# A two-layer fp32 backbone: the second layer's first MLP product made of seven block products

## The chip, the core and the metric

The kernel runs on one core of a Trainium2 chip. The metric is the device time of one execution in microseconds (us): the median of three runs of the kernel before is 2430.54 us (2429.8 to 2430.73). A matrix product runs on TensorE (PE in the rows; PEld is its weight load), elementwise work on VectorE (DVE), ScalarE (ACT) and GpSimd (POOL); SyncE (SP) issues most transfers.

## The reference

Two layers work on 1024 latent tokens of width 1024, with 256 context tokens beside them in the first. Each layer has a token mixer (Fourier mixing in layer 0, windowed attention in layer 1) and then a squared-ReLU MLP. Only layer 1's MLP is computed in a new way; it has no context tokens.

```python
def _sq_relu_mlp(h, w1, w2):
    return jnp.square(jax.nn.relu(h @ w1)) @ w2     # w1: 1024 x 4096, w2: 4096 x 1024
...
h_lat = h_lat + g2 * _sq_relu_mlp(_modulate(_rms_norm(h_lat, norm2_g[i]), sh2, sc2), mlp_w1[i], mlp_w2[i])
```

Everything is fp32. Each operand of a product is split into a rounded high part and the rest (`h` and `l` in the names), and a product is three matmuls: high by high, high by low, low by high (`mm3`, L51 to L53). ScalarE makes the high part with a copy; VectorE or GpSimd makes the low part with a subtraction (`lo_part`, L58).

## The kernel before

`layer_tail` runs for both layers: it projects the mixer's output (`project`, weights `l_ph`, `l_pl`), adds it to the residual `ht`, normalises into `nh` and `nl`, and runs the MLP. The tokens stand in two blocks of 512 (b = 0, 1), in layer 0 also a block of 256 context tokens. The 4096 hidden columns are taken in 16 pairs of 128-column chunks. For one pair:

- hidden: four units, each one chunk of w1 by one token block, 8 steps over the width of three matmuls with 512 columns: 24 matmuls a unit, 96 a pair. A unit's result stands in a PSUM bank `l_z_ps`. ScalarE takes the positive part into `l_slot` (`relu`, L953), VectorE multiplies it by the bank's positive part (`square`, L1254).
- outputs: the second product is already a seven-product (Strassen-Winograd) scheme. The 2 x 2 blocks are w2's two row chunks and its two halves of columns against the hidden blocks B11, B12, B21, B22. VectorE makes the sums of w2 (`summed`, L1291) and the differences T1 to T4 of the hidden blocks (`diff`, L1268), ScalarE and VectorE split them (`high` L964, `low` L58 into `l_al`). A product is 4 groups of three matmuls (L1589 to L1591), 84 matmuls a pair; group m writes the PSUM bank `l_yy_ps`m.
- read-out: the running sum in `l_yy_ps` is read after each product. Banks 0 to 2 are read by VectorE (`acc`, L1275), bank 3 by ScalarE (`side_read`, L971) and then added by GpSimd (`add`, L862). The next product's group m waits until bank m has been read (`freed`).

So there is one product of time between a group and its successor on the same bank. Each engine runs its own list in the order in which it is written (the bodies below `@block.vector` and so on), and waits on semaphores. In layer 1 the order of the products is M5, M3, M1, M6, M7, M4, M2, with M5 before the last hidden unit, B21.

In layer 0 GpSimd's list for a pair is `outputs(p, more)`: add M5, the low part of S2, add M3, the low part of w1's chunk 0 (`low1`), the low part of S3, add M2, add M1, the low parts of A22 and A21, `low1` of chunk 1, then the adds of M6, M7 and M4. The context product (`l_yc_ps`) in four groups waits for weight low parts; its third group, ahead of M4, needs those of A22 and A21. SyncE's list is `pair(r, ...)`: w1 chunks of the next pair, the six ada transfers of this pair (`load_a`, each released by a step of VectorE), w2 of the next pair, two ada transfers of the next.

## Time and profile before

| | |
|---|---|
| median of the runs | 2430.54 us |
| span of the profiled execution, first to last instruction | 2428.1 us |
| around the span, median less span | 2.4 us |
| PE / DVE / ACT / POOL busy | 94% / 72% / 45% / 42% |
| stage of layer 0's MLP | about 321 to 1165 us, 16 pairs |
| stage of layer 1's MLP | about 1750 to 2426 us, 16 pairs |

The page shows each engine's busy share over 40 slices and TensorE's granted clock in tenths. It is read from the top: who is full, where, and at which clock; then the timeline of single engines within one pair of each layer, which repeats.

### The profile page before, as it was taken

The page shows a single profiled execution, that of the slowest core. Times are in us where ns is not written, and L with a number is a line of the kernel's source. Part 1 is how long each engine was busy: PE and PEld are TensorE (multiplying, and loading weights), DVE is VectorE, ACT ScalarE, POOL GpSimd, SP SyncE. Part 2 cuts the span into 40 slices and gives each one's busy share as a digit, 9 for nine tenths or more (in the row PEclk, how much of TensorE's full clock was granted, in tenths as well). Part 3 has the DMA queues.
Part 4 walks back from the last instruction along what each step waited for, and adds up shares of the span by engine and source line. Part 5 has one row for each costly group of instructions (what it writes and reads, how often), then busy time and mean ns, then how long its engine had stood idle before and what let it go on. Part 6 is the DMA issues. An engine that isn't in the chain of part 4 may idle for free. (4 is left out here: it accounts for less than half of the span.)

```text
span 2428.1 us, 36937 instructions
## 1 busy us (share of the span) xinstructions
PE 2281.3 (94%) x11598; PEld 1900.3 (78%) x11598; DVE 1736.5 (72%) x2835; ACT 1100.7 (45%) x1985; POOL 1022.5 (42%) x816
## 2 busy tenths in 40 slices
PE   5989979999999999999699799888999999999998
PEld 3768868888888888888687677766778888888887
DVE  5653787777777777777774688871688787878776
ACT  5553443333333333333443588882343444444443
POOL 0003623433333443333656476765435353545443
PEclk9999999999999999999799899999999999999999
DMA  7434112222222222222212211104111111121212
GB/s 272 176 130 174 66 35 70 86 87 72 84 78 69 70 82 98 69 80 88 105 53 109 81 36 34 35 22 191 44 35 53 51 46 57 37 67 35 69 35 96
DMA packets 79297, 192.75 MB, mean 79 GB/s; under 512 B 6896, under 2 KB 15472, under 8 KB 75888
## 3 DMA queue, kind: packets, MB, share of 16 engines
q1 hardware_dynamic: 76288, 184.92, 22.4%
q10 hardware_dynamic: 2928, 6.82, 0.8%
q8 instruction: 42, 0.69, 0.1%
q14 instruction: 39, 0.32, 0.0%
HBM read 174.94 MB, written 16.78 MB: 79 GB/s over the span
## 5 line engine op out<-in xcount | busy, mean ns | idle before, releaser
L862 POOL TENSOR_TENSOR ht<-ht,l_side 128x512 f32<-128x512 f32 x224 | 301.3, 1345 | 919.2 <-ACT l_side L971 910.8
L1275 DVE SCALAR_TENSOR_TENSOR ht<-l_yy_ps,mod,ht 128x512 f32<-128x512 f32 x672 | 466.1, 743 | 26.9 <-PE l_yy_ps L1591 26.0
L51 PE MATMUL l_z_ps<-nh,l_w1h 128*128 128x512 f32 (+1 forms) x1280 | 474.2, 370 | 11.7 <-DVE nl L1215 6.3
L52 PE MATMUL l_z_ps<-nl,l_w1h 128*128 128x512 f32 (+1 forms) x1280 | 473.2, 370 | 0.0
L53 PE MATMUL l_z_ps<-nh,l_w1l 128*128 128x512 f32 (+1 forms) x1280 | 472.6, 369 | 0.0
L1589 PE MATMUL l_yy_ps<-l_ah,l_w2h 128*128 128x512 f32 x896 | 355.6, 397 | 9.8 <-DVE ht L1275 6.9
L1590 PE MATMUL l_yy_ps<-l_al,l_w2h 128*128 128x512 f32 x896 | 351.0, 392 | 0.0
L1591 PE MATMUL l_yy_ps<-l_ah,l_w2l 128*128 128x512 f32 x896 | 350.5, 391 | 0.0
L971 ACT ACTIVATE l_side<-l_yy_ps,mod 128x512 f32<-128x512 f32 x224 | 154.1, 688 | 335.2 <-PE l_yy_ps L1591 335.2
L51 PEld LDWEIGHTS l_z_ps<-nh,l_w1h 128*128 128x128 f32 x1280 | 242.4, 189 | 54.5 <-issue 7.6
L53 PEld LDWEIGHTS l_z_ps<-nh,l_w1l 128*128 128x128 f32 x1280 | 242.5, 189 | 40.7
L52 PEld LDWEIGHTS l_z_ps<-nl,l_w1h 128*128 128x128 f32 x1280 | 242.5, 189 | 40.6 <-issue 0.5
L964 ACT ACTIVATE l_ah<-l_slot 128x512 fp32r<-128x512 f32 x224 | 141.6, 632 | 232.3 <-DVE l_slot L1254 93.4
L58 DVE TENSOR_TENSOR l_al<-l_slot,l_ah 128x512 fp32r<-128x512 f32 x224 | 185.8, 829 | 58.5 <-ACT l_ah L964 56.6
L1589 PEld LDWEIGHTS l_yy_ps<-l_ah,l_w2h 128*128 128x128 f32 x896 | 169.4, 189 | 50.3 <-DVE ht L1275 9.8
L1591 PEld LDWEIGHTS l_yy_ps<-l_ah,l_w2l 128*128 128x128 f32 x896 | 169.1, 189 | 36.4
L1590 PEld LDWEIGHTS l_yy_ps<-l_al,l_w2h 128*128 128x128 f32 x896 | 169.7, 189 | 31.8
L945 ACT ACTIVATE l_w2h<-l_w2f 128x512 fp32r<-128x512 f32 x240 | 141.7, 621 | 101.0 <-DVE l_w2f L1291 90.2
L2303 POOL TENSOR_TENSOR sc<-sc,den 128x640 f32<-128x640 f32 (+1 forms) x128 | 149.6, 1202 | 89.3 <-DVE den L2385 89.3
L58 POOL TENSOR_TENSOR l_w1l<-l_w1f,l_w1h 128x1024 fp32r<-128x1024 f32 x64 | 168.0, 2626 | 0.0
L58 POOL TENSOR_TENSOR l_w2l<-l_w2f,l_w2h 128x512 fp32r<-128x512 f32 x112 | 152.7, 1369 | 3.6 <-ACT l_w2h L945 3.5
L58 POOL TENSOR_TENSOR l_pl<-early,l_ph 128x1024 fp32r<-128x1024 f32 x20 | 49.4, 2473 | 247.9 <-ACT l_ph L1025 247.9
(250 smaller groups left out, 4515.5 us busy)
## 6 DMA issues: line engine op xcount, KB each, us to landing
l_aw<-ada SPq DMA_DIRECT2D x128, 256.0 KB, 2.9
l_w1f<-w SPq DMA_DIRECT2D x64, 512.0 KB, 3.5
l_w2f<-w SPq DMA_DIRECT2D x64, 512.0 KB, 4.9
maw<-ada SPq DMA_DIRECT2D x24, 1024.0 KB, 5.3
queries<-qhl SPq DMA_DIRECT2D x16, 512.0 KB, 2.8
stage<-queries SPq DMA_DIRECT2D x32, 256.0 KB, 2.7
early<-fnet_w SPq DMA_DIRECT2D x11, 512.0 KB, 4.5
early<-wo SPq DMA_DIRECT2D x11, 512.0 KB, 3.5
```

Of the source, the lines that this page charges most:

```text
L51: pe.matmul(out, lh, rh, start=first, stop=False)
L52: pe.matmul(out, lh, rl, start=False, stop=False)
L53: return pe.matmul(out, ll, rh, start=False, stop=last)
L58: return eng.tensor_tensor(lo, full, f32(hi), ALU.subtract)
L862: pool.tensor_tensor(h, h, side[(i - 1) % 2][:], ALU.add).then_inc(s_add, 1)
L945: act.activation(w2h[:, RING[name]], w2f[:, PLACE[name]], ACT.Copy).then_inc(s_w2h, 1)
L971: act.activation(side[(i - 1) % 2][:], y_ps[SIDE][:], ACT.Copy, scale=mod[:, layer, G2, m, 0:1]).then_inc(s_ya, 1)
L1275: dve.scalar_tensor_tensor(out=h, in0=y_ps[m][:], scalar=mod[:, layer, G2, c, 0:1], in1=h, op0=ALU.mult, op1=ALU.add).then_inc(s_acc, 1)
L1589: pe.matmul(y_ps[m][:], wh, a_h, start=first, stop=False, skip_group_check=not first)
L1590: pe.matmul(y_ps[m][:], wh, a_l, start=False, stop=False, skip_group_check=not first)
L1591: pe.matmul(y_ps[m][:], wl, a_h, start=False, stop=True, skip_group_check=not first).then_inc(s_y, 1)
L2303: pool.tensor_tensor(row, row, den[:, i, h:h + 1].to_broadcast(list(row.shape)), ALU.mult).then_inc(s_p, 1)
```

## The change

Layer 1's tail is a new function, `strassen_tail`. Its pairs 0 and 1 make the hidden blocks plainly, as before (`plain_block`). In pairs 2 to 15 the hidden product too is seven block products: the blocks are w1's two chunks by the two halves of the width, against the normalised tokens' halves of width and their two blocks. Each product is 4 steps of three matmuls, 12 matmuls, 84 a pair.

- The sums of layer 1's w1 and w2 are made during layer 0's MLP by transfers between DRAM tensors into the new tensor `sums`: in each of layer 0's 16 pairs SyncE issues four copies of 512 KB (`start_sums`), and GpSimd issues four transfers that add to their destination (`first_sums` twice, `more_sums` S2 and S4), with waits on the copies and on each other.
- The sums of the tokens are made once, in pair 1, on VectorE (16 instructions, `third_sum`, `first_sum`, `second_sum`, `fourth_sum`), and split (`high_t`, `low_t`: 16 on ScalarE, 12 on VectorE, 4 on GpSimd).
- The hidden products run in the order M1, M5, M6, M2, M7, M3, M4, accumulate in three banks, are copied by ScalarE in between (`copied`: 3 a pair) and summed by VectorE into PSUM (`zsum`: 3 a pair). The squared blocks and differences stand partly in PSUM, so that their low parts are read from there.
- The second product runs in the order M1, M6, M7, M4, M5, M3, M2, all of it after the hidden products. VectorE makes three of its seven low weight parts, GpSimd four; its sums are loaded, not made.

```diff
+            Z_ORDER = ["M1", "M5", "M6", "M2", "M7", "M3", "M4"]
+            Y_ORDER = ["M1", "M6", "M7", "M4", "M5", "M3", "M2"]
...
+                def first_sums(p):
...
+                    pool.wait_ge(s_sc, p * 64 + 64)
+                    pool.dma_start(sums[0, 0:2, to]..., w1[1, one, 1]..., accum_op=ALU.add, max_dma_last_dim=2048).then_inc(s_s1, 16)
+                    pool.dma_start(sums[1, 0:2, to]..., w2[1, chunks, :, 512:1024]..., accum_op=ALU.add, max_dma_last_dim=2048).then_inc(s_s1, 16)
...
+                def more_sums(p, name):
...
+                    if name == "S2":
+                        pool.wait_ge(s_s1, p * 32 + 32)
...
                     add(p, "M3")
+                    if C:
+                        first_sums(p)
                     if more and C:
                         low1(p + 1, 0)
                     low2(p, "S3")
                     for prod in ROWS[2:]:
                         add(p, prod)
+                        if C and prod in ("M2", "M7"):
+                            more_sums(p, "S2" if prod == "M2" else "S4")
...
+                if C:
+                    pool.wait_ge(s_s4, 16 * PAIRS)
...
+                def group(p, i, m):
...
+                    if m == SIDE:
+                        pe.wait_ge(s_ya, p * 7 + (PRE + i))
+                    else:
+                        pe.wait_ge(s_acc, p * 21 + (PRE + 3 * i + m - 2))
...
+                def last_sums(p, side_sums):
+                    diff(p, "T2")
+                    diff(p, "T3")
+                    low(p, "T2")
+                    low(p, "T3")
+                    acc(p, 0, 0)
+                    acc(p, 0, 1)
+                    if not (type(p) is int and p == 0):
+                        square(p, "B21")
+                    diff(p, "T4")
+                    low(p, "T1")
+                    acc(p, 0, 2)
+                    low(p, "T4")
+                    acc(p, 1, 0)
+                    low(p, "B22")
+                    acc(p, 1, 1)
+                    acc(p, 1, 2)
+                    acc(p, 2, 0)
+                    low(p, "B21")
...
+                def pair(p):
+                    for i in (0, 1, 2):
+                        low2(p, i)
+                    zsum(p, "B11")
+                    square(p, "B11")
+                    low(p, "B11")
+                    zsum(p, "B22")
+                    square(p, "B22")
+                    zsum(p, "B12")
+                    square(p, "B12")
+                    diff(p, "T1")
+                    last_sums(p, False)
```

## Rows read from the trace of the kernel before

**Rows 1.** The page: busy time by engine; granted clock in 40 slices.

```profile
PE 2281.3 (94%) x11598; PEld 1900.3 (78%) x11598; DVE 1736.5 (72%) x2835; ACT 1100.7 (45%) x1985; POOL 1022.5 (42%) x816
PEclk9999999999999999999799899999999999999999
```

**Rows 2.** Stretches: length, busy us of each engine (instructions), PEclk, DMA share, GB/s.

```profile
350.00:1090.00 740.00, 734.08 (x3887) 634.12 (x3888) 561.21 (x899) 268.71 (x446) 268.54 (x182) 1.00 0.24 78
1862.00:1903.00 41.00, 41.00 (x182) 33.77 (x181) 32.08 (x45) 17.04 (x28) 19.08 (x12) 1.00 0.15 51
```

**Rows 3.** Timeline, PE in layer 1: start us, duration us, instruction.

```profile
1863.34 0.39 PE L51 MATMUL l_z_ps<-nh,l_w1h 128*128 128x512 f32 x1
1864.02 0.39 PE L51 MATMUL l_z_ps<-nh,l_w1h 128*128 128x512 f32 x1
```

**Rows 4.** Timeline, DVE, a pair of layer 1: start, duration, idle before.

```profile
1859.37 0.74 DVE L1275 SCALAR_TENSOR_TENSOR ht<-l_yy_ps,mod,ht 128x512 f32<-128x512 f32 x1
...
1898.31 0.69 DVE L1254 SCALAR_TENSOR_TENSOR l_slot<-l_z_ps,l_slot 128x512 f32<-128x512 f32 x1 [1.60 <-ACT l_slot L953]
1899.04 0.69 DVE L1268 TENSOR_TENSOR l_slot<-l_slot 128x512 f32<-128x512 f32 x1
...
1900.31 0.74 DVE L1275 SCALAR_TENSOR_TENSOR ht<-l_yy_ps,mod,ht 128x512 f32<-128x512 f32 x1
1900.97 0.68 DVE L1268 TENSOR_TENSOR l_slot<-l_slot 128x512 f32<-128x512 f32 x1
1901.57 0.68 DVE L58 TENSOR_TENSOR l_al<-l_slot,l_ah 128x512 fp32r<-128x512 f32 x1
...
1903.50 1.40 DVE L58 TENSOR_TENSOR l_al<-l_slot,l_ah 128x512 fp32r<-128x512 f32 x1
1907.08 2.06 DVE L1275 SCALAR_TENSOR_TENSOR ht<-l_yy_ps,mod,ht 128x512 f32<-128x512 f32 x3
```

**Rows 5.** Timeline, ACT, the same pair: positive part, high part, side read.

```profile
1905.84 0.60 ACT L953 ACTIVATE l_slot<-l_z_ps 128x512 f32<-128x512 f32 x1 [2.42 <-PE l_z_ps L53]
1907.20 0.63 ACT L964 ACTIVATE l_ah<-l_slot 128x512 fp32r<-128x512 f32 x1 [0.76 <-PE l_yy_ps L1591]
```

**Rows 6.** Timeline, POOL in layer 1: an add and a low part.

```profile
1903.06 1.29 POOL L862 TENSOR_TENSOR ht<-ht,l_side 128x512 f32<-128x512 f32 x1 [17.19 <-ACT l_side L971]
1904.31 1.73 POOL L58 TENSOR_TENSOR l_w2l<-l_w2f,l_w2h 128x512 fp32r<-128x512 f32 x1
```

**Rows 7.** Timeline, PE at layer 1's first pair; a stretch behind its wait.

```profile
1777.15 0.47 PE L1589 MATMUL l_yy_ps<-l_ah,l_w2h 128*128 128x512 f32 x1 [2.94 <-DVE l_al L58]
1778.60:1781.70 3.10, 2.73 (x7) 1.61 (x5) 3.00 (x6) 2.24 (x4) 0.00 (x0) 0.51 0.00 0
```

**Rows 8.** Timeline, POOL in a pair of layer 0, and the next pair's first.

```profile
841.65 1.30 POOL L862 TENSOR_TENSOR ht<-ht,l_side 128x512 f32<-128x512 f32 x1 [31.88 <-ACT l_side L971]
...
845.40 2.90 POOL L58 TENSOR_TENSOR l_w1l<-l_w1f,l_w1h 128x1024 fp32r<-128x1024 f32 x1
849.49 2.76 POOL L862 TENSOR_TENSOR ht<-ht,l_side 128x512 f32<-128x512 f32 x2
852.20 2.56 POOL L58 TENSOR_TENSOR l_w2l<-l_w2f,l_w2h 128x512 fp32r<-128x512 f32 x2
895.00 1.30 POOL L862 TENSOR_TENSOR ht<-ht,l_side 128x512 f32<-128x512 f32 x1 [31.88 <-ACT l_side L971]
```

**Rows 9.** Timeline, PE in that pair: the third context group starts.

```profile
856.61 0.28 PE L51 MATMUL l_yc_ps<-l_ach,l_w2h 128*128 128x256 f32 x1
```

**Rows 10.** Transfers: an issue on SP; sizes and us to landing; a wait.

```profile
857.64 0.33 SPq L767 DMA_DIRECT2D l_w1f<-w  x1
l_w2f<-w SPq DMA_DIRECT2D x64, 512.0 KB, 4.9
881.95 0.75 DVE L1242 SCALAR_TENSOR_TENSOR l_side<-l_aw,l_sseq,l_side 128x512 f32<-128x512 f32 x1 [0.87 <-DMA l_aw<-ada]
```

More of the change, by code:

```diff
@@ L58, in lo_part, with hybrid_kernel @@
     return eng.tensor_tensor(lo, full, f32(hi), ALU.subtract)
-def hybrid_kernel(nc, x, ctxt, vecs, ada0, ada1, w1, w2, fnet_w, wqkv, wo, qkg, sink, dft, rope, masks, eye, out, park, qd):
+def hybrid_kernel(nc, x, ctxt, vecs, ada0, ada1, w1, w2, fnet_w, wqkv, wo, qkg, sink, dft, rope, masks, eye, out, park, qd, sums):
     ctx = ExitStack()
@@ L70, in sem @@
             return s
+        s_sums = [ctx.enter_context(nc.semaphore(n)) for n in ("sums13", "sums2", "sums4")]
         def recycle_semaphores():
@@ L561, in layer_tail @@
 def layer_tail(nc, sem, sb, banks, layer, wp, early, s_pw, w1, w2, mod, meanw, eps, ident, nh, nl, ht,
-               x=None, ctxt=None, g1b=None, ada1=None, vec=None, svec=None, ones=None, kv=None, sqs=None, park=None, out=None):
+               x=None, ctxt=None, g1b=None, ada1=None, vec=None, svec=None, ones=None, kv=None, sqs=None, sums=None, s_sums=None, park=None, out=None):
     PAIRS = DFF // (2 * P)
@@ L2561 @@
     qd = nc.dram_tensor("queries", (QB, HEADS // 4, P, 4 * 2 * HD), F32, kind="Internal").ap()
-    hybrid_kernel(nc, *args, out, park, qd)
+    sums = nc.dram_tensor("sums", (2, 4, 1 + DFF // (2 * P), P, 512), F32, kind="Internal").ap()
+    hybrid_kernel(nc, *args, out, park, qd, sums)
     r = run_bass_kernel_spmd(nc, [arrays], core_ids=[0])
```

903 lines of the change are left out of this document (901 added, 2 removed).

## The prediction

> **What bounds the kernel now.** I read the page's busy shares first: TensorE is busy for 94% of the span and its clock is near full nearly everywhere [rows 1]. Then the stretches: in both MLP stages TensorE has no idle time to speak of (734 of 740 us in layer 0, 41.0 of 41.0 in layer 1) at a granted clock of 1.00, its higher level, 2.4 GHz [rows 2]. So in both stages every microsecond that TensorE loses is a microsecond of the kernel, and every matmul less is a gain only as long as nobody else makes TensorE wait. In layer 1 three matmuls start within 0.68 us, 0.2267 each [rows 3], and a pair repeats after 1900.31 - 1859.37 = 40.94 us [rows 4]: 180 x 0.2267 = 40.81 and 0.13 of rest. VectorE is next, busy 32.1 of 41 [rows 2]. A page of shares hides the order within a pair, so I then followed each engine's timeline through a pair, since the change rearranges just that.
>
> **What the change removes.** In pairs 2 to 15 the hidden product has 84 matmuls for 96: 12 x 0.2267 = 2.72 us a pair, 14 pairs, 38.1 us. That is the whole gain, and a pair would take 168 x 0.2267 = 38.08 us.
>
> **What it does to VectorE in layer 1.** VectorE had 44 instructions a pair (21 read-outs, 7 low parts of operands, 4 squares, 4 differences, 4 weight sums, 4 weight low parts) and has 42 (three `zsum`, three weight low parts, the rest as before). Independent ones start 0.60 us apart (1900.97, 1901.57), a read-out takes 2.06/3, or 0.66 from the next, and one that needs its forerunner starts 0.73 behind it (1898.31, 1899.04) [rows 4]. 42 of them are some 27 us, so as a sum VectorE fits into 38 us. But their places have changed. Before, M5 ran between two hidden units, and the differences had that time. Now all hidden products come first, and M1, M6, M7, M4 follow without a gap, each group waiting for the read-out of the same bank one product (2.72 us) earlier.
>
> I work it through from the start of a pair's M1 (0). Product k of the hidden seven ends at 2.72k + 0.17 (a matmul ends 0.39 behind its start [rows 3]), and the next engine starts 0.03 later. The sixth, M3, ends at 16.49. Then VectorE `zsum` B12 16.52 to 17.21; ScalarE's positive part, 0.60 [rows 5], to 17.84; square to 18.56; T1 18.60; T2 19.32; T3 19.92; the high part of T2 on ScalarE, 0.63 [rows 5], to 20.67; low T2 20.70, low T3 21.30 to 21.98, first read-out 21.90 to 22.64. TensorE has finished M1's groups at 21.76 and can't start M6's first before 22.67: 0.9 lost. The second read-out ends at 23.30, in time. The third stands behind square B21 (23.2), T4 (23.9, behind it by dependence) and low T1 (24.5), and runs 25.15 to 25.89. M6's third group needed it at 24.03: 1.9 lost. Then low T4, read-out M6/0 to 27.15, low B22, read-out M6/1 to 28.41, where M7's second group needed it at 27.96: 0.5 lost. From M7's third group on the read-outs keep up (0.66 each against 0.68 a group). M4 starts at 30.48 where 27.20 was due, and the pair ends at 41.36. So the stall is 3.28 us and eats the 2.72: 41.36 - 40.94 = +0.42 a pair.
>
> VectorE's instructions that read and write PSUM both don't occur before; the nearest rows are those that read one operand from PSUM, 0.69 [rows 4]. I take these; 0.60 for each of the 13 in the chain (7.8 us and 1.2 for ScalarE's two) or 0.75 would make the pair 40.8 or 42. Where both its operands stand in SBUF, VectorE can be held by GpSimd: low parts take 1.40 for 0.69 now and then [rows 4], and GpSimd's 1.73 for 1.3 [rows 6]. Low T1 (24.5) falls on GpSimd's low part of M4's weights (about 23.5 to 24.8): +0.3, taken at half, +0.13. Layer 1's loop: 14 x 0.55 = +7.7 us (bounds -2 to +15).
>
> The Trainium skill (SBUF — State Buffer, Who interferes with whom) says that a VectorE instruction with two SBUF inputs contends with a GpSimd instruction that reads SBUF and one with at most one does not. The trace agrees, since read-outs from PSUM stay at 0.74 beside GpSimd. It speaks for blocks in PSUM, and leaves the order as it is.
>
> ScalarE (35 instructions, about 0.6 each, 22 us) and GpSimd (18, about 1.3, 24 us) fit into 41, their results each come over 1 us before they are needed, and w1's and w2's 14 transfers of 256 KB a pair are issued 3 us or more ahead of use: nothing.
>
> **Layer 1's first two pairs.** Pair 0 has lost 2.94 and two short waits, and then ran at 0.51 of the clock, the lower level, for 3.1 us [rows 7]. In the new order M1 can start at 1774.1, but the stall of the loop follows (4.6 us until M4): it ends near 1797.7, 1.6 earlier than now. In pair 1 VectorE has 16 token sums and 12 low parts more, 28 x 0.65 = 18 us. The sums fill its list to about 19 us, so that T2 and T3 come late: the first read-out ends at 28.3 where TensorE is ready at 24.5, the pattern above adds 2.4, and the low parts of T1 and T3 behind the read-outs of M4 and M5 add 0.6 and 1.7. +8.5 us (bounds +3 to +14, the latter if the clock falls once more). Layer 1 together: 7.7 - 1.6 + 8.5 = +14.6.
>
> **Layer 0.** GpSimd's list gets four transfers. None is issued by GpSimd in the trace, so their cost on it has bounds: 0.33 us, an issue on SyncE [rows 10], and 2.9, its longest instruction here [rows 8]. I take 1.3, an ordinary instruction of its own [rows 6]. From 841.65 GpSimd has no idle time until it has made A22 and A21 at 854.76; the third context group starts at 856.61 [rows 8, 9]. Slack 1.85 us. Three issues stand ahead (two behind M3's add, one behind M2's): 3.9 - 1.85 = 2.05 us a pair. TensorE is the bound, so it counts, in pairs 1 to 14 (pair 0 has idle time on GpSimd, pair 15 no `low1`): 29 us. In front of the third issue GpSimd waits for the first two to land. The second is issued until 848.1; GpSimd gets there at 848.1 + 5.4 = 853.5, so 5.4 us are covered; a plain load of this size lands in 4.9 [rows 10]. An addition moves three times for two, so it may take up to 9.8, and the wait 0 to 4.4; I take 0. Behind the wait stand the adds, which free the side buffers two products later, and A22 and A21. SyncE's four copies cost it 1.6 us and put 2 MB ahead of the next w1 chunk, which has 20 us; they would hit the ada transfers, for which VectorE waits 0.87 already [rows 10], only if they lasted over 14 us. At the end GpSimd waits for the last S4: +3 us. Layer 0 together +32 (bounds +3 to +130).
>
> The Trainium skill (DMA: Bandwidth & Descriptors, Specifications) puts the first byte of a transfer issued by GpSimd at about 1 us; by that estimate three issues less the slack are 1.15 a pair, 16 us for the 29. No row of this trace shows it.
>
> **Sum.** The profiled execution's span is 2428.1, and 2.4 us lie around it, against the median of 2430.5. 2428.1 + 14.6 + 32 + 2.4 = 2477 us.
>
> **Rivals.**
> Forecast: VectorE's list takes back the seven products' gain, and GpSimd's issues cost layer 0 29 us. 2477, chance 0.33.
> Cheap issues: an issue takes under 0.6 us on GpSimd and lies in the slack. For it: SyncE's 0.33. Against: GpSimd does nothing else in under 1.2. 2430.5 + 14.6 + 3 = 2448, chance 0.21.
> Late landings: the additions land in about 8.4 us, 3 us of wait for each of 14 pairs on top, 42 us. For it: each reads two sources and writes DRAM, beside w1's and w2's loads. 2519, chance 0.18. The clock belongs here too: stalls of 3 us have cost it before [rows 7], mine are at most 1.9 each.
> Faster: TensorE stays full in layer 1's loop. Its place is M6's third group, and it decides where the third read-out ends, 23.9 and not 25.9. Then 14 x 2.72 = 38 is kept, pair 1 costs 4, layer 0 its 3: 2430.5 - 38 - 1.6 + 4 + 3 = 2398. For it: VectorE's total fits with 11 us to spare, layer 0 may be free. Against: 13 instructions in 7 us were never seen. Chance 0.22.
> The change does the seven products, but a cheaper stall (2.7 in place of 3.3, pair 1 at +3) and free issues just cancel: 2431, chance 0.06.
>
> **How the numbers follow.** Likeliest is 2477. The range goes from the faster rival's time to just over the late landings, 2396 to 2525; beyond it lie late landings with the full 9.8 us and a faster case without pair 1's loss. Faster by over 0.2% (4.9 us, about what a measurement can tell from no change) 0.22, within 0.06, slower 0.72. The likeliest side's own range is 2440 to 2525.
>
> **What would show it.** In the loop of layer 1: a period of 41.4 to 41.6 us (38.1 by the faster rival), waits of TensorE at the second product's second, third and fourth group sets for VectorE's `ht` of about 0.9, 1.9 and 0.5 us, and VectorE without idle time from `zsum` B12 to M4's read-outs. In layer 0: a period over the 53.35 of now [rows 8] by 2 us, and a wait of TensorE at the third context group for GpSimd's low parts. If layer 0's period stays 53.35 the issue price was wrong; if layer 1's falls under 40, the order of VectorE's chain was.

## The result and the profile after

The changed kernel takes 2566.3 us (median of four runs, 2564.0 to 2568.6), the kernel before 2430.2 (2429.5 to 2430.7): 1.0555 times as long, 95% interval 1.054 to 1.057. The direction was forecast, the size was not: 136 us slower, where 47 had been worked out and 2525 us was the end of the range.

The page of the kernel after, the rows that answer to [rows 1] (span; busy us of an engine, share, instructions; granted clock in 40 slices):

```profile
span 2567.1 us, 38476 instructions
PE 2319.5 (90%) x11430; PEld 1908.2 (74%) x11430; DVE 1731.1 (67%) x2827; ACT 1155.4 (45%) x2117; POOL 1155.5 (45%) x974
PEclk9999989999999999999889899999989999999999
```

TensorE has 168 matmuls fewer in the list, is busy for longer all the same (2319.5 us for 2281.3) and has 101 us more of idle time. A busy time that rises with fewer instructions means a slower clock. So two things are to be found, waits and half clock, and the first question is in which stage.

The last projection matmul (tile l_ph) starts at 1743.4 in the trace of before and at 1829.5 in that of after: 86.1 us are lost before layer 1's MLP begins, and the remaining 139.0 - 86.1 = 52.9 in it. The stretches, as in [rows 2] (length, busy us and instructions of PE, PEld, DVE, ACT, POOL, then clock, DMA share, GB/s). First layer 0's MLP and one of its pairs, then a pair of layer 1:

```profile
350.00:1230.00 880.00, 830.02 (x4216) 707.90 (x4215) 614.80 (x979) 290.84 (x483) 345.59 (x255) 0.96 0.53 141
828.80:887.08 58.28, 55.47 (x285) 47.25 (x284) 40.70 (x66) 19.31 (x33) 22.98 (x17) 0.97 0.55 144
2074.80:2118.60 43.80, 40.46 (x170) 32.43 (x169) 29.70 (x42) 20.28 (x35) 23.43 (x18) 0.96 0.27 84
```

A pair of layer 0 takes 58.28 us where 53.35 stood [rows 8], and it was forecast at 55.4. A pair of layer 1 takes 43.8 where 40.94 stood [rows 4], and 41.5 was forecast. In both the clock is no longer 1.00. The pair shown is one of the shorter: layer 0's fourteen loop pairs take 58.0 to 60.1 us, 58.60 in the mean, and make 73 of the 86 us. Layer 1's (42.9 to 44.0, mean 43.80) make 40 of the 53.

**A pair of layer 0, GpSimd** (start us, duration, instruction, idle time before it and what ended it), to be laid beside [rows 8]:

```profile
832.55 1.03 POOL L909 DMA_DIRECT2D sums<-w  x1
833.29 1.46 POOL L910 DMA_DIRECT2D sums<-w  x1
834.00 3.19 POOL L58 TENSOR_TENSOR l_w1l<-l_w1f,l_w1h 128x1024 fp32r<-128x1024 f32 x1
836.37 2.06 POOL L58 TENSOR_TENSOR l_w2l<-l_w2f,l_w2h 128x512 fp32r<-128x512 f32 x1
837.62 2.06 POOL L881 TENSOR_TENSOR ht<-ht,l_side 128x512 f32<-128x512 f32 x1
841.88 1.15 POOL L922 DMA_DIRECT2D sums<-sums  x1 [2.20 <-DMA sums<-w]
842.64 1.70 POOL L881 TENSOR_TENSOR ht<-ht,l_side 128x512 f32<-128x512 f32 x1
843.88 2.90 POOL L58 TENSOR_TENSOR l_w2l<-l_w2f,l_w2h 128x512 fp32r<-128x512 f32 x2
```

An issue holds GpSimd for about 0.74 us (832.55, 833.29, 834.00), not the 1.3 of the sum. But the third stands behind 2.20 us of waiting for the first two to land (1.9 to 3.1 in the fourteen pairs), and only behind it come the low parts of A22 and A21. The transfers in this stage (count, size of each, median us to landing):

```profile
sums<-w POOLq DMA_DIRECT2D x30, 512.0 KB, 7.3
sums<-sums POOLq DMA_DIRECT2D x30, 512.0 KB, 6.0
l_w2f<-w SPq DMA_DIRECT2D x30, 512.0 KB, 4.2
```

An addition lands in 7.3 us, a load of the same size in 4.2. TensorE's timeline in the same pair, at its two waits:

```profile
844.08 0.50 PE L1635 MATMUL l_yy_ps<-l_ah,l_w2h 128*128 128x512 f32 x1 [0.84 <-ACT l_side L1017]
847.03 0.36 PE L51 MATMUL l_yc_ps<-l_ach,l_w2h 128*128 128x256 f32 x1 [1.97 <-POOL l_w2l L58]
```

The second is the wait for GpSimd's low parts, for which the landing wait stands in front. The first has another cause, which ScalarE's and SyncE's rows show. TensorE waits for a side read-out, and ScalarE, which reads it, has first waited 2.75 us for the load of w1's second chunk:

```profile
842.40 1.06 ACT L984 ACTIVATE l_w1h<-l_w1f 128x1024 fp32r<-128x1024 f32 x1 [2.75 <-DMA l_w1f<-w]
843.36 0.67 ACT L1017 ACTIVATE l_side<-l_yy_ps,mod 128x512 f32<-128x512 f32 x1
837.35 0.33 SPq L771 DMA_DIRECT2D l_w1f<-w  x1
l_w1f<-w SPq DMA_DIRECT2D x1, 512.0 KB, 5.0
```

The same load in the pair of before that starts at 841.65, where ScalarE doesn't wait for it (its copy starts at 852.40):

```profile
848.46 0.33 SPq L767 DMA_DIRECT2D l_w1f<-w  x1
l_w1f<-w SPq DMA_DIRECT2D x1, 512.0 KB, 3.4
```

Both chunks use one buffer, so this load is issued when GpSimd has made chunk 0's low part (`load1` waits for it). That low part stands behind the first two issues: the load goes out 8.55 us behind the pair's first GpSimd instruction, where it was 6.81. And it lands in 5.0 us, not 3.4, beside the additions. Together it comes 3.3 us later. ScalarE had 0.5 us to spare for it; TensorE, further down, about 2.3, since 1.0 of the 3.3 reaches it.

The stretch behind the second wait (columns as above):

```profile
849.00:851.50 2.50, 2.50 (x7) 1.92 (x7) 1.63 (x3) 0.00 (x0) 2.36 (x3) 0.50 1.04 371
```

The gap between starts is 1.00 us over the usual 0.23 at the first wait and 2.14 at the second. From 848.2 on three narrower matmuls (256 columns) start 0.17 to 0.22 apart, not 0.12, six of 512 columns 0.43 apart and a seventh 0.37, not 0.23: 1.6 us more, since the granted clock is 0.50, the lower level of 1.2 GHz. With two starts that are 0.1 late behind a wait this is 4.9, the whole 4.93 of the pair.

**A pair of layer 1, VectorE** from the `zsum` of B12 on. Its pair's first matmul started at 2070.66:

```profile
2087.48 0.70 DVE L2452 TENSOR_TENSOR l_z_ps<-l_z_ps,l_slot 128x512 f32<-128x512 f32 x1
2088.84 0.69 DVE L2459 SCALAR_TENSOR_TENSOR l_slot<-l_z_ps,l_slot 128x512 f32<-128x512 f32 x1 [0.66 <-ACT l_slot L2177]
2089.57 0.69 DVE L2469 TENSOR_TENSOR l_slot<-l_z_ps,l_slot 128x512 f32<-128x512 f32 x1
2090.29 0.69 DVE L2473 SCALAR_TENSOR_TENSOR l_slot<-l_slot,l_z_ps 128x512 f32<-128x512 f32 x1
2090.90 0.69 DVE L2476 TENSOR_TENSOR l_z_ps<-l_z_ps,l_slot 128x512 f32<-128x512 f32 x1
2091.68 0.69 DVE L58 TENSOR_TENSOR l_al<-l_slot,l_ah 128x512 fp32r<-128x512 f32 x1
2092.29 0.68 DVE L58 TENSOR_TENSOR l_al<-l_z_ps,l_ah 128x512 fp32r<-128x512 f32 x1
2092.89 1.40 DVE L2491 SCALAR_TENSOR_TENSOR ht<-l_yy_ps,mod,ht 128x512 f32<-128x512 f32 x2
2094.20 0.69 DVE L2462 SCALAR_TENSOR_TENSOR l_z_ps<-l_z_ps,l_slot 128x512 f32<-128x512 f32 x1
2095.00 0.69 DVE L2480 SCALAR_TENSOR_TENSOR l_z_ps<-l_slot,l_z_ps 128x512 f32<-128x512 f32 x1
2095.61 1.50 DVE L58 TENSOR_TENSOR l_al<-l_slot,l_ah 128x512 fp32r<-128x512 f32 x1
2097.03 0.74 DVE L2491 SCALAR_TENSOR_TENSOR ht<-l_yy_ps,mod,ht 128x512 f32<-128x512 f32 x1
```

(The square of B22 stands at 2086.65, just ahead of it.) And TensorE, which waits for the read-outs in the first and the last `ht` row above:

```profile
2093.85 0.49 PE L2662 MATMUL l_yy_ps<-l_ah,l_w2h 128*128 128x512 f32 x1 [1.01 <-DVE ht L2491]
2097.82 0.79 PE L2662 MATMUL l_yy_ps<-l_ah,l_w2h 128*128 128x512 f32 x1 [2.33 <-DVE ht L2491]
```

The stretch behind the second:

```profile
2097.90:2100.90 3.00, 3.00 (x7) 2.40 (x8) 3.00 (x5) 0.11 (x1) 0.33 (x1) 0.50 0.47 175
```

Again by gaps between starts: 1.18 and 0.10 at the first wait, 2.48 at the second, and 0.36, five times 0.20 and 0.17 while the clock is 0.50, 1.5 us. Together 5.3, and 38.5 for the rest, the 168 matmuls' own 38.1 among them, make the period of 43.8. All pairs of the loop have these two waits, but two of thirteen have no half clock behind them:

```profile
2027.77:2070.66 42.89, 39.42 (x170) 31.20 (x168) 29.57 (x43) 20.27 (x35) 23.43 (x18) 1.00 0.28 86
```

So the half clock costs such a pair 1.1 us net (44.0 for 42.9): at full clock a third, shorter wait shows, which the half clock covers.

### The profile page after: what moved, and what is told of

It is laid out like the page before. It is cut to its first block and busy times, and to the rows that moved or that the text cites. A ratio compares the mean times of both kernels' runs of the same rounds, so it can differ in the third digit from the quotient of the medians.

```text
span 2567.1 us, 38476 instructions
## 1 busy us (share of the span) xinstructions
PE 2319.5 (90%) x11430; PEld 1908.2 (74%) x11430; DVE 1731.1 (67%) x2827; ACT 1155.4 (45%) x2117; POOL 1155.5 (45%) x974
## 5 line engine op out<-in xcount | busy, mean ns | idle before, releaser
L51 PE MATMUL l_z_ps<-nh,l_w1h 128*128 128x512 f32 (+1 forms) x816 | 292.9, 359 | 6.6 <-POOL l_w1l L58 3.4
L53 PE MATMUL l_z_ps<-nh,l_w1l 128*128 128x512 f32 (+1 forms) x816 | 291.8, 358 | 0.0
L52 PE MATMUL l_z_ps<-nl,l_w1h 128*128 128x512 f32 (+1 forms) x800 | 285.8, 357 | 0.0
L1321 DVE SCALAR_TENSOR_TENSOR ht<-l_yy_ps,mod,ht 128x512 f32<-128x512 f32 x336 | 235.9, 745 | 20.6 <-PE l_yy_ps L1637 19.2
L58 POOL TENSOR_TENSOR l_w1l<-early,l_w1h 128x512 fp32r<-128x512 f32 x104 | 135.6, 1311 | 179.7 <-ACT l_w1h L2149 179.7
L1635 PE MATMUL l_yy_ps<-l_ah,l_w2h 128*128 128x512 f32 x448 | 187.0, 417 | 22.3 <-ACT l_side L1017 14.6
L51 PEld LDWEIGHTS l_z_ps<-nh,l_w1h 128*128 128x128 f32 x816 | 154.8, 190 | 30.4 <-issue 4.0
L1017 ACT ACTIVATE l_side<-l_yy_ps,mod 128x512 f32<-128x512 f32 x112 | 76.6, 684 | 214.8 <-PE l_yy_ps L1637 214.8
L53 PEld LDWEIGHTS l_z_ps<-nh,l_w1l 128*128 128x128 f32 x816 | 154.9, 190 | 22.4
L52 PEld LDWEIGHTS l_z_ps<-nl,l_w1h 128*128 128x128 f32 x800 | 152.0, 190 | 22.0 <-issue 0.5
L2662 PEld LDWEIGHTS l_yy_ps<-l_ah,l_w2h 128*128 128x128 f32 x448 | 90.1, 201 | 97.1 <-DVE ht L2491 58.4
L2491 DVE SCALAR_TENSOR_TENSOR ht<-l_yy_ps,mod,ht 128x512 f32<-128x512 f32 x192 | 136.3, 745 | 24.2 <-PE l_yy_ps L2664 24.2
```

Source lines behind the costliest of these rows:

```text
L51: pe.matmul(out, lh, rh, start=first, stop=False)
L52: pe.matmul(out, lh, rl, start=False, stop=False)
L53: return pe.matmul(out, ll, rh, start=False, stop=last)
L58: return eng.tensor_tensor(lo, full, f32(hi), ALU.subtract)
L1321: dve.scalar_tensor_tensor(out=h, in0=y_ps[m][:], scalar=mod[:, layer, G2, c, 0:1], in1=h, op0=ALU.mult, op1=ALU.add).then_inc(s_acc, 1)
L1635: pe.matmul(y_ps[m][:], wh, a_h, start=first, stop=False, skip_group_check=not first)
```

## The experiments

After the traces I had this theory (P in the first four expectations): each stage loses by itself, layer 0 by where the additions stand in GpSimd's list, layer 1 by where the read-outs stand in VectorE's; the traffic of the sums as such costs little. The rivals: one stage disturbs the other, or the traffic and the issues cost whatever their place.

**sums_alone.** The additions as in the kernel after, layer 1's MLP as before (the sums are made and not used).

```diff
-        strassen_tail(..., w1, w2, sums, ...)
+        layer_tail(nc, sem, sb, banks, 1, wo, early, s_pw, w1, w2, ...)
```

> The kernel before with layer 0's sum transfers added, layer 1's MLP as before (the sums are not read). Theory P (what the trace of the changed kernel shows: in each middle pair of layer 0 TensorE waits behind GpSimd, which itself waits 2.2 us for the first additions to land; the pair goes from 53.35 to 58.28 us; the two stages are independent): 15 x 4.93 plus the end of the layer, 86 us up to the last projection of layer 1, so 2430 + 86 = 2516 us, and layer 1's MLP as long as before. Rival I (the stages act on each other, for example through the clock or through what the transfers leave behind): under 2495 or over 2535 us.

Measured 2514.6 us, 1.034 of before (1.031 to 1.037): layer 0 costs 82 us by itself (before took 2432.6 beside it). The last projection matmul starts at 1831.2, as in the kernel after (1829.5).

**layer1_alone.** No copies and no additions; layer 1 with its seven products, which loads a plain block of the same size for each sum (so the weight sums are left out).

```diff
-                        start_sums(r)
...
-                        first_sums(p)
...
-                            more_sums(p, "S2" if prod == "M2" else "S4")
```

> The changed kernel without any sum transfers; layer 1 loads plain blocks of w1 and w2 of the same size in place of the sums, so what it computes in layer 1 leaves the sums of weights out. Theory P: layer 0 as before (53.35 a pair), layer 1's MLP as long as in the changed kernel, period 43.8, total 2430 + 51 = 2481 us. Rival I: layer 1's period falls clearly under 43 us, since the stall came from loads of the sums.

Measured 2482.6, 1.021 (1.018 to 1.024), and the last projection matmul starts at 1742.5, as before (1743.4). Layer 1 costs 50 us by itself, and 82 + 50 = 132 of the 136 for both. So the two parts are separate and can be explained one by one.

**first_only.** The first additions stay, S2 and S4 are left out.

```diff
-                        if C and prod in ("M2", "M7"):
-                            more_sums(p, "S2" if prod == "M2" else "S4")
```

> As sums_alone, but the two second-stage transfers (S2, S4) are left out: GpSimd issues only the two additions of the first stage and waits for nothing inside the pair. Theory P (it is the wait for the landing and the third issue that use up the slack of 1.85 us; an issue holds GpSimd 0.74 us): 2 x 0.74 = 1.5 us fits into the slack, layer 0's pair stays at 53.4, total 2430 to 2436 us. The prediction's price of 1.3 us an issue: 2.6 - 1.85 = 0.75 a pair, 2440 to 2446 us. Rival D (the DRAM traffic itself slows layer 0): the pair stays near 57 to 58 us, over 2490 us.

(The sums S2 and S4 are not made.) Measured 2464.9, 1.013 (1.011 to 1.016). Layer 1 is as before here too, so layer 0's cost falls from 82 to 32 us. That is none of the numbers expected. The trace shows two things. In an ordinary pair (period 54.5) TensorE waits 0.9 us for a side read-out (ScalarE l_side, 11.7 us in 13 waits), and ScalarE again waits for w1's second chunk first, which lands in 5.0 us (50.3 us of such waits in 14 pairs). And in 3 of the 16 pairs, the 4th, 8th and 11th, GpSimd's second issue is held:

```profile
920.56 1.02 POOL L909 DMA_DIRECT2D sums<-w  x1
926.69 1.15 POOL L910 DMA_DIRECT2D sums<-w  x1 [5.12 <-issue]
```

From one issue to the next it is 6.13 us where 0.73 is usual; such a pair takes 58.5 to 58.9 us for 54.5. Fourteen pairs at 1.1 and three holds at 4.2 are 29 of the 32 us. In the kernel after no pair has a hold: its second issue starts 0.73 to 0.87 behind the first in all 16. So the holds belong to this variant and are no part of the 136 us.

**first_small.** first_only with half the memory for GpSimd's descriptors.

```diff
-    nc = bacc.Bacc("TRN2", ..., dynamic_dma_scratch_size=4096)
+    nc = bacc.Bacc("TRN2", ..., dynamic_dma_scratch_size=2048)
```

> The kernel with the first additions alone (S2 and S4 left out, so these two sums are not made: part of the computation is missing), with the memory for GpSimd's transfer descriptors halved, 2048 bytes for 4096. In three of its sixteen pairs (the 4th, 8th and 11th) GpSimd's second issue was held for 5.1 to 5.5 us and the pair took 58.5 to 58.9 us for 54.5. Theory V (a new transfer has to wait for room among the descriptors of the one in flight): with half the room at least six pairs are held, 2465 rises by 4.3 for each, to 2478 or more, up to 2520 when every pair is. Rival (the hold has nothing to do with that memory): three holds again, 2461 to 2469.

Measured 2484.7, 1.021 (1.020 to 1.023): 20 us more, and six pairs held for three, by 5.2 to 5.7 us each (427.83, 541.19, 600.88, 769.84, 938.61, 1108.29). So the hold depends on that memory. More than 4096 bytes was not tried. Why the hold falls on the 8th, 16th and 22nd transfer, and why the kernel after has none, is open.

**second_later.** All transfers, but S2's issue behind the low parts of A22 and A21, and S4's behind the pair's last addition.

```diff
                         add(p, prod)
-                        if C and prod in ("M2", "M7"):
-                            more_sums(p, "S2" if prod == "M2" else "S4")
...
                         if prod == "M1":
                             for name in W_LATE[2:]:
                                 low2(p, name)
                             if more:
                                 low1(p + 1, 1 if C else 0)
+                            if C:
+                                more_sums(p, "S2")
+                    if C:
+                        more_sums(p, "S4")
```

> The kernel after, with GpSimd's issue of the second addition (S2) put behind the low parts of A22 and A21, and of the third (S4) behind the last addition of the pair; the same transfers in all. In the kernel after GpSimd waits 2.20 us there for the first additions to land and spends about 0.75 on the issue, all ahead of the low parts that TensorE waits 2.0 for. Theory L (what failed in the sum for layer 0 is the wait for landing, priced at nothing): the waits of TensorE for l_w2l vanish, the period of a pair of layer 0 falls from 58.28 to 54.4 to 55.6, where the kernel with the first additions alone stands (54.47), time 2566 less 38 to 54: 2512 to 2528. Rival I (the issues and the traffic themselves hold the pair, wherever they stand): period 57 or more, time over 2548.

Measured 2511.6, 1.033 (1.031 to 1.034): 54.8 us of the kernel after's 136 come back by moving two issues. In the trace the first additions have landed when GpSimd gets to S2 (873.63 in the pair below, without a wait), all waits of TensorE for l_w2l in the loop are gone, and the half clock with them in thirteen of fourteen pairs. TensorE's wait that is left:

```profile
871.84 0.50 PE L1637 MATMUL l_yy_ps<-l_ah,l_w2h 128*128 128x512 f32 x1 [0.89 <-ACT l_side L1019]
```

And the pair as a stretch:

```profile
860.27:914.79 54.52, 53.63 (x286) 46.09 (x285) 40.43 (x66) 19.37 (x32) 23.19 (x19) 1.00 0.57 154
```

3.76 us of the pair's 4.93 are gone (by the means of fourteen pairs 58.60 has become 54.93). On TensorE that is the second wait with its late start, 2.2, and the half clock, 1.6. The remaining 1.17 is the wait of 0.89 for l_side and its surroundings, with ScalarE waiting for w1's second chunk as in the kernel after (43.3 us in 14 pairs). The adds that free the side buffers are not the cause: the last add ahead of that read-out ends at 868.85, and ScalarE reads at 871.11, right behind its copy of the late chunk. The odd pair is of use for the clock: its one wait of 1.97 for l_side (982.10) has the half clock behind it, and the pair takes 57.1 us.

**sums_in_idle.** All issues where GpSimd has nothing to do, behind the pair's last addition; the copies behind the ada transfers. The last pair stays as it was.

```diff
-                    if C:
+                    if C and not more:
                         first_sums(p)
...
-                        if C and prod in ("M2", "M7"):
+                        if C and not more and prod in ("M2", "M7"):
                             more_sums(p, "S2" if prod == "M2" else "S4")
...
                     if more and not C:
                         low1(p + 1, 1)
+                    if more and C:
+                        first_sums(p)
+                        more_sums(p, "S2")
+                        more_sums(p, "S4")
```

> The changed kernel with layer 0's additions of a pair moved behind GpSimd's last add of that pair, where it stands idle for 32 us (the last pair as it was), and SyncE's copies moved behind the six ada transfers. All sums are made. Theory P (a matter of place, not of traffic): layer 0's pair back to 53.4 us, total within 6 us of layer1_alone, about 2485 us. Rival D (traffic): layer 0's pair stays over 56 us, total over 2525 us.

Measured 2496.8, 1.027 (1.024 to 1.030): 70 of the kernel after's 136 us are back, and 14 over layer1_alone stay, 12 over the time expected. GpSimd's third and fourth issue in a pair (the first two start at 923.27 and 924.01):

```profile
932.45 1.14 POOL L922 DMA_DIRECT2D sums<-sums  x1 [6.96 <-DMA sums<-w]
940.84 1.14 POOL L922 DMA_DIRECT2D sums<-sums  x1 [7.25 <-DMA sums<-sums]
```

A pair as a stretch:

```profile
901.87:955.22 53.35, 53.35 (x285) 46.19 (x284) 40.19 (x66) 19.31 (x33) 23.55 (x17) 1.00 0.59 157
```

In this pair and eight more of the fourteen the period is before's 53.35 [rows 8], with twice the bytes moved (157 GB/s for 79). GpSimd now waits 7 us twice and it costs nothing, and ScalarE waits for w1 nowhere: its second chunk is issued as early as before and lands in 3.6 us. So it was the place of issues and traffic that cost nearly all of it. The traffic isn't quite free: an ada transfer lands in 4.8 us for 2.9, VectorE's waits for l_aw double from 19.3 to 41.7 us in all, and five pairs are 0.4 to 1.2 us longer because TensorE waits for VectorE's ada step, 3.4 us together. The 14 us that stay are before layer 1 (last projection matmul at 1757.5, 14.1 behind before's): 3.5 up to the loop, 3.4 in it, and 7 behind it, of which 4.5 are the last pair's wait for l_w2l.

**third_read_early.** From here on the kernels are about layer 1. The third read-out of the first product right behind the second:

```diff
                     acc(p, 0, 1)
+                    acc(p, 0, 2)
                     if not (type(p) is int and p == 0):
                         square(p, "B21")
                     diff(p, "T4")
                     low(p, "T1")
-                    acc(p, 0, 2)
```

> The kernel after, with one operation of VectorE's order moved in layer 1's MLP: the third read-out of a pair's first product (l_yy_ps bank 2) is done right after the second, ahead of the last block's square, of T4 and of the low part of T1. In the kernel after the read-out starts 26.35 us behind the pair's first matmul and TensorE waits 2.33 for it; moved ahead of three operations of 0.60, 0.73 and 1.50 us it should start at about 23.5 and that wait be gone. Theory Q (VectorE's order sets the loop of layer 1, and the half clock follows the two waits): the period of the loop falls from 43.81 to between 40.3 and 42.0 (some of the three moved operations then make the third product late instead, 0.5 to 1.5 us), fourteen pairs and pair 1, so 2566 falls to 2515 to 2543. Rival R (the half clock at this place comes from something else than the second wait, the time of that wait only being given back later, at T4): the half clock stretch stays, the period is 42.5 or more, time over 2546. Rival N (the loop is set by GpSimd's low parts or loads): no change, 2560 to 2570.

Measured 2549.6, 1.048 (1.046 to 1.050): 17 us gained. That is outside what theory Q said, and both the time (over 2546) and the mean period (43.1, R said 42.5 or more) are R's. The trace explains it. The wait of 2.33 at M6's third group is gone, and one of 1.76 at M7's first group has come, for M6's first read-out, which still stands behind the square, T4 and the low parts of T1 and T4. And the clock does two different things in two successive pairs with the same waits (1.02 and 1.76 in one, 1.01 and 1.76 in the next):

```profile
2067.07:2110.90 43.83, 40.93 (x170) 32.45 (x169) 29.01 (x42) 20.16 (x35) 23.50 (x18) 0.96 0.28 84
2110.90:2153.39 42.49, 39.59 (x170) 31.34 (x169) 29.08 (x42) 20.16 (x35) 23.47 (x18) 1.00 0.28 86
```

43.83 against 42.49: the half clock costs 1.34 us by itself here. Over the loop, seven of thirteen pairs have it (43.6 to 44.0) and six don't (42.3 to 42.5).

**fill_waits.** The order of the kernel after, but TensorE multiplies low parts by low parts where it would wait.

```diff
                     pe.matmul(y_ps[m][:], wh, a_l, start=False, stop=False, ...)
+                    if not is_plain(p):
+                        for _ in range({(0, 3): 3, (1, 1): 9}.get((i, m), 0)):
+                            pe.matmul(y_ps[m][:], wl, a_l, start=False, stop=False, ...)
```

> The kernel after, with twelve more matmuls of 0.23 us (low parts times low parts, a term the kernel leaves out as too small to matter, repeated) in each pair of layer 1's loop: three at the end of the first product and nine in the second group of the second product, just where TensorE waits 1.01 and 2.33 us in the kernel after. They fill 0.68 of the first wait and 2.04 of the second, so nothing that TensorE waits for comes later. Theory Q (the half clock of 3 us follows from the waits): TensorE is busy in their place, the granted clock stays above 0.95 through the stretch, and the period falls from 43.81 by the 1.3 to 1.9 us that the half clock costs, to 41.9 to 42.5; fourteen pairs, 2566 falls to 2540 to 2548. Rival R (the half clock comes from elsewhere, for example from what all matmuls together draw): clock as before, period 43.8 or more, time 2564 to 2575; more matmuls would then even make it worse.

Measured 2552.5, 1.049 (1.047 to 1.051): 14 us faster with 168 matmuls more. A pair as a stretch:

```profile
2071.65:2114.55 42.90, 42.12 (x182) 33.44 (x181) 29.60 (x42) 20.39 (x35) 23.51 (x19) 1.00 0.28 85
```

Of its two waits on TensorE the first is 0.33 (2090.71) and the second:

```profile
2094.74 0.50 PE L2662 MATMUL l_yy_ps<-l_ah,l_w2h 128*128 128x512 f32 x1 [0.32 <-DVE ht L2491]
```

The clock stays at 1.00 in every pair of the loop, so the half clock does follow the waits. Both the time and the period are above what theory Q expected. The period is that of the kernel after's two pairs at full clock (42.9), so the gain is 1.1 us in each of the others and not 1.5, because at full clock TensorE reaches M7's groups earlier and meets another late read-out there (M7's second group, 0.53 behind its forerunner, 0.30 over the usual). In the kernel after, the half clock hides this third wait; the two pairs without it show it.

**reads_between.** VectorE's whole order dealt anew, T4's parts ahead of T1's, ScalarE's side read-out of M6 ahead of T4's high part; the same operations.

```diff
                     diff(p, "T2")
-                    diff(p, "T3")
-                    low(p, "T2")
-                    low(p, "T3")
                     acc(p, 0, 0)
+                    low(p, "T2")
                     acc(p, 0, 1)
+                    acc(p, 0, 2)
+                    diff(p, "T3")
+                    acc(p, 1, 0)
+                    low(p, "T3")
+                    acc(p, 1, 1)
+                    acc(p, 1, 2)
                     if not (type(p) is int and p == 0):
                         square(p, "B21")
                     diff(p, "T4")
...
```

> The kernel after, with VectorE's order in layer 1's MLP dealt anew: each read-out of the first three products stands ahead of the operation that the next product doesn't need yet (T2, read, low T2, read, read, T3, read, low T3, read, read, square, T4, read, low T4, read, read, low T1), T4's parts are made before T1's, and ScalarE reads the second product's side chunk before it makes the high part of T4. The same operations, all of them. Theory Q: with 0.60 to 0.70 us each, the first two products' groups find their banks read; the fourth product waits about 1.2 us for the low part of T4; period 39.5 to 40.8 in place of 43.81, 14 pairs, and 2 to 5 us in pairs 0 and 1: 2566 falls to 2503 to 2524. Rival W (the work of VectorE between the third block's square and the fourth product is too much in any order, and the waits only move): one wait of 2.5 us or more at the fourth product with half clock behind it, period 42 or more, time over 2540.

Measured 2525.5, 1.039 (1.038 to 1.041): 41 us gained, 1.5 short of what theory Q expected. M4's wait of 1.2 isn't there; another stands at M6's fourth group, for ScalarE. The period is 40.94 and the clock 1.00:

```profile
2063.52:2104.46 40.94, 39.32 (x170) 31.25 (x169) 29.24 (x42) 20.30 (x35) 23.36 (x18) 1.00 0.30 90
```

TensorE's largest wait in it:

```profile
2084.81 0.51 PE L2664 MATMUL l_yy_ps<-l_ah,l_w2h 128*128 128x512 f32 x1 [1.18 <-ACT l_side L2194]
```

**reads_between_idle** has both moves, this order and the additions in GpSimd's idle time.

> The last kernel (VectorE's order dealt anew in layer 1's MLP) with the additions of the sums put into GpSimd's idle time at the end of each pair of layer 0 and their copies behind the loads. If the two edits are in stages that don't touch each other, their gains add: 2497 (sums_in_idle) less what the new order alone gains against the kernel after (43 to 63 us expected): 2434 to 2454, no faster than the kernel before. If the order of layer 1 gains more than 66 us, the block products beat the kernel before (2430).

Measured 2457.3, 1.011 (1.009 to 1.013). From 2496.8 to 2457.3 are 39.5 us, from 2566.3 to 2525.5 are 40.8: the gains add, and before isn't reached.

**reads_between_idle2.** ScalarE's side read-out of the first product ahead of T3's high part.

```diff
                     high(p, "T2")
+                    side_read(p, 0)
                     high(p, "T3")
...
-                    side_read(p, 0)
```

> reads_between_idle with one more move: ScalarE reads the side chunk of a pair's first product (l_side) ahead of making T3's high part, which waits for VectorE. In reads_between TensorE waited 1.18 us in each pair of layer 1's loop for that read-out, the largest wait left there. If nothing else is late behind it: period 40.94 falls to 39.7 to 40.0, in 14 pairs 13 to 17 us, 2457 falls to 2440 to 2444, still slower than before. If the next wait (0.43 for VectorE's read-out) takes it over: 2448 or more.

Measured 2457.3, 1.011 (1.009 to 1.012): nothing. The period is 40.97, the wait of 1.18 for ScalarE is gone, and one of 1.03 for VectorE stands at M4's first group. The wait:

```profile
2015.90 0.50 PE L2668 MATMUL l_yy_ps<-l_ah,l_w2h 128*128 128x512 f32 x1 [1.03 <-DVE l_al L58]
```

The first and the last two of VectorE's instructions ahead of it, which have no idle time between them:

```profile
2005.68 0.69 DVE L2473 TENSOR_TENSOR l_slot<-l_z_ps,l_slot 128x512 f32<-128x512 f32 x1
...
2014.40 0.75 DVE L2495 SCALAR_TENSOR_TENSOR ht<-l_yy_ps,l_gneg,ht 128x512 f32<-128x512 f32 x1
2015.15 0.69 DVE L58 TENSOR_TENSOR l_al<-l_z_ps,l_ah 128x512 fp32r<-128x512 f32 x1
```

From T1 to T4's low part, which M4's first group needs, these are 15 instructions in 10.2 us (2005.68 to 2015.84), and TensorE is through with its own work 1.03 earlier. Each of the 15 is needed by M4's first group or by a group ahead of it, so an order within them can only move that wait. This is the second kernel in which it moved and the period stayed. Giving one of the 15 to another engine was not tried.

**last_pair_late.** The last pair's additions are moved to GpSimd's list in layer 1, behind pair 0.

```diff
-                    if C and not more:
-                        first_sums(p)
...
+                sp.wait_ge(s_sums[2], 16 * PAIRS)
                 with sp.Fori(PLAIN, PAIRS - 1) as p:
```

> reads_between_idle2 with the additions of the last pair (the one pair whose additions still stand among GpSimd's low parts in layer 0) done in layer 1 instead, in GpSimd's order behind pair 0; its sums are first loaded twelve pairs later. TensorE's wait of 4.5 us for l_w2l at the last pair of layer 0 should go, and some of the wait behind it: 4 to 8 us faster than reads_between_idle2, so 2433 to 2439, within 0.4% of before but not under it. If more than 8 us come back, it is level with the kernel before.

Measured 2449.3, 1.008 (1.006 to 1.009): 8 us faster than the last one, the upper end of the gain expected (the time expected was lower, as it built on the last one's). It is the best version with block products, 117 us faster than the kernel after, and the kernel before is still faster by 18.

## Why the prediction was wrong

By its own steps, the number forecast and the number found:

| step | forecast | found |
|---|---|---|
| issue on GpSimd | 1.3 each | 0.74 each (6.1 in three pairs of first_only, in none of the kernel after) |
| landing of the first additions | within 5.4 us, no wait | 7.3 median, a wait of 2.20 |
| w1's second chunk, ScalarE, side read-out | not in the sum | 3.3 us later, TensorE waits 0.84 |
| layer 0, a loop pair | +2.05 | +5.25 in the mean (+4.93 in the pair shown) |
| layer 0 in all | +32 (bounds +3 to +130) | +82 alone, +86 beside layer 1 |
| first read-out of M1's groups | 21.90 | 22.23 |
| third read-out | 25.15 | 26.37 |
| waits at M6's groups | 0.9 and 1.9 | 1.01 and 2.33 |
| clock behind them | full | 0.50 for 3 us, in 11 of 13 pairs |
| layer 1, a loop pair | +0.55 | +2.87 |
| layer 1 in all | +14.6 | +50 alone, +53 beside layer 0 |

**Mechanism and size.** The sign was right, and so was the mechanism in layer 1, the place of the read-outs. In layer 0 the engine was right, GpSimd's list, but not what in it costs: the sum had the three issues, and the trace has the wait between them, a second chain behind the first two, and the clock. The two terms came out 2.6 and 3.4 times as large. The steps that failed:

**The landing wait, taken as 0.** I had bounds of 0 to 4.4 and 5.4 us of cover. The additions of the pair above took until 841.9 with an issue at 833.3, 8.6 us. The cover was as forecast: GpSimd came to the wait 5.7 us behind the second issue's end. I took the end of the bounds that lies nearest to a plain load (4.9 us), though I had written down myself that an addition moves three times for two: 1.5 x 4.9 = 7.35 would have been the estimate, and 7.3 is what was measured. With it the wait is about 2 us (7.35 - 5.4), 27 us more for the sum: about 2504, an estimate by the prediction's own numbers and still 62 short. The rival of late landings (2519) named this mechanism; it had 0.18. second_later shows that it was the largest part of layer 0's loss: with the half clock behind it, 54.8 us came back.

**The issue price** was too high (1.3 for 0.74), an error the other way: three issues are 2.2 us, little more than the slack of 1.85. **The second chain** wasn't in the sum at all. I measured the slack of one consumer of GpSimd's list only, the low parts of A22 and A21 (1.85 us). Chunk 0's low part stands behind the first two issues as well, and on it hang the load of w1's second chunk, ScalarE's copy of it and the side read-out behind that copy. The load went out 1.7 us later and took 1.6 longer (5.0 for 3.4) beside the additions, and TensorE could bear about 2.3. By this estimate neither would have cost it anything alone, but no run parts the two. TensorE's 0.84 to 0.9 us stand in first_only and second_later too, and are gone in sums_in_idle, where neither stands ahead of the load.

The Trainium skill (DMA: Bandwidth & Descriptors, Specifications) gave about 1 us for a transfer's first byte by GpSimd. For what GpSimd itself is held the trace has 0.74; for the time until an addition of 512 KB has landed it has 6.0 to 7.3. The first number says nothing of either, and the estimate by it, 16 us for layer 0, was further off than the 29 from the rows.

**The clock** failed in both stages. I wrote that stalls of 3 us have cost it before and that mine are at most 1.9 each, and left it in a rival for layer 0 alone. In both stages the trace shows two waits within 4 us (0.84 and 1.97; 1.01 and 2.33) and then about 3 us at 0.50. In layer 0 all fourteen pairs have it (two of them for longer), and by the gaps between starts it costs about 1.7 us a pair, 24 us (an estimate from these gaps); second_later took the larger wait away, and the clock went back to 1.00 in all pairs but one. In layer 1 fill_waits kept VectorE's times, filled the waits, had 1.00 in every pair, and was 14 us faster. Together some 38 us that stood nowhere in the sum. It is no sharp rule of the waits' sizes: two pairs of layer 1 with the same waits kept the full clock, six of third_read_early with 1.0 and 1.8 too, while a single wait of 1.97 brought the half clock in a pair of second_later.

**VectorE's chain in layer 1** was followed rightly: seven operations after `zsum` B12, each came 0.3 us later than worked out, as `zsum` itself stood behind the square of B22 (2086.65, 2087.48), and operations that read and write PSUM take 0.69 to 0.70, the value taken. The term for the contention was too small. Low T1 fell on GpSimd's low part as forecast, and took 1.50 us in place of 0.69; I had taken half of 0.3. The Trainium skill (SBUF — State Buffer, Who interferes with whom) says that a VectorE instruction with two SBUF inputs contends with a GpSimd instruction that reads SBUF, and that one with at most one does not. The trace agrees: low T1, with slot and high part in SBUF, is the only one in the list above that is lengthened, and low T4 behind it, which reads PSUM, takes 0.68 (2097.69) although GpSimd's add runs beside it (2096.51, for 1.72). The rule names who is hit; it was for me to take the price from the row of before, 0.7 more [rows 4], in full.

The third wait, 0.5 in the sum, at M7, is there at 0.3, and most pairs of the kernel after don't show it: the half clock covers it. It appears as soon as the clock is full (fill_waits).

**The rivals.** Cheap issues (2448) had an issue under 0.6 us; 0.74 is nearer to it than to the sum's 1.3, but its result was wrong, since the wait for landing and the late load stand behind the issues. Faster (2398) hung on the third read-out's end; in third_read_early TensorE no longer waited for it, and the late group was another one. reads_between_idle2 shows why: the limit is the sum of VectorE's work in that stretch and not one read-out's place. So a kernel in which the seven products keep their 38 us didn't exist in any order of the same operations that I tried. The best loop of layer 1 has the period of before (40.94), with 12 matmuls less a pair, all of them turned into waits. That the two figures are the same is chance as far as the traces show: before, TensorE's matmuls filled the period; here they fill 39.3 us of it, and waits for VectorE and ScalarE the rest.

**What stays open.** Pairs 0 and 1 of layer 1, with the ends of the loop, have the remaining 53 - 40 = 13 us (waits of 6.24 and 3.91 for VectorE's read-outs in pair 1, half clock behind both); I had +6.9 for them and changed nothing there by itself. Of layer 0's 86 us 13 lie outside the loop's fourteen pairs, 4 up to it and 9 behind; last_pair_late gave back 8. How much of the late load is the issues' and how much the traffic's isn't parted. What makes the clock fall or stay in two like pairs isn't settled.

## What to carry to other kernels

Where a list of work goes on an engine behind a wait, price the wait and then every chain that hangs on the list behind it, not only the tightest one that comes to mind: here two low parts had 1.85 us of slack, and a third, which frees a load buffer that ScalarE's list waits for, had about 2.3, of which a slower transfer took 1.6. Some 18 us later in the same list, behind the pair's last addition, the same transfers cost next to nothing. Taking 7% of the bound engine's work away pays only as far as the other engines can do theirs in the shorter time between two points, so add up their work between those points, and not over the period. And where waits of 1 to 2.5 us follow close on each other, add what they may cost in clock, 1.1 to 1.8 us a time here.

## What the hardware showed beyond that

- Twice the traffic was nearly free: with the issues in idle time, layer 0 moved 157 GB/s for 79 at an unchanged period of 53.35 us in nine of fourteen pairs; the other five lost 3.4 us together to late ada transfers (4.8 us to land for 2.9).
- In the wrong place it isn't: a 512 KB load beside the additions took 5.0 us for 3.4 and made ScalarE, and then TensorE, wait.
- An accumulating transfer of 512 KB from DRAM to DRAM by GpSimd lands in 6.0 to 7.3 us (median), 8.6 in the pair shown, and holds GpSimd for 0.74.
- The issue right behind another one can be held for 5.1 to 5.7 us, in 3 of 16 pairs with 4096 bytes of descriptor memory and in 6 of 16 with 2048.
- TensorE's granted clock fell to 0.50 for about 3 us behind two waits of 0.84 and 1.97 us that lie 3 us apart, with TensorE busy all the time before and between them; behind waits of 1.0 and 2.33 it fell in 11 of 13 like pairs. Twelve useless matmuls a pair in the place of two such waits made the kernel 14 us faster.
